# One accumulating transfer for two output tiles, and a second half that borrows the gate and up copies' tile

## The reference, cut to what matters

```
x = x + 0.5 * (silu(rms(x) @ gate1) * (rms(x) @ up1)) @ down1     # first feed-forward
x = x + mixer(rms(x))                                             # untouched
x = x + 0.5 * (silu(rms(x) @ gate2) * (rms(x) @ up2)) @ down2     # second feed-forward
y = rms(x)
```

## Time and profile of the kernel before

| what | value |
|---|---|
| median of 3 runs | 2687.12 us (2686.59 to 2691.2) |
| the profiled execution | 2686.25 us, of which its span is 2684.4 us |
| mean granted TensorE clock | 0.971 of full speed |
| TensorE matmul / VectorE / ScalarE / GpSimd busy | 95% / 64% / 50% / 11% |
| DMA: GpSimd's queue, SyncE's queue | 84.56 MB in 21.3%, 185.11 MB in 20.8% of the 16 engines' span |

### The profile page before, as it was taken

How to read it: one execution, slowest core, us unless ns; L and a number is a source line. 1 busy time by engine, 2 the same in 40 slices (tenths; PEclk the granted TensorE clock), 3 DMA queues, 4 the chain that set the end, 5 groups by cost and what they waited for, 6 DMA issues and landing times.

```text
span 2684.4 us, 52562 instructions
## 1 busy us (share of the span) xinstructions
PE 2538.3 (95%) x19577; PEld 2495.5 (93%) x19577; DVE 1710.4 (64%) x2897; ACT 1337.5 (50%) x2323; POOL 300.1 (11%) x346
## 2 busy tenths in 40 slices
PE   8999999999989999999999999999999999989997
PEld 7999999999978999999999999999999999989997
DVE  6766666666668766766666765542675666666666
ACT  5344444444447667666565664211534444444444
POOL 0012112221230000000000000000101122212220
PEclk9999999999999999999999999999999999999999
DMA  3356656555551112221221215432035656555565
GB/s 116 111 99 111 109 107 108 105 107 106 108 168 64 59 63 73 70 73 56 88 102 64 102 68 200 147 123 81 25 111 99 110 106 109 103 105 109 106 110 162
DMA packets 98984, 271.10 MB, mean 101 GB/s; under 512 B 10304, under 2 KB 16832, under 8 KB 98368
## 3 DMA queue, kind: packets, MB, share of 16 engines
q0 software_dynamic: 43648, 84.56, 21.3%
q1 hardware_dynamic: 55232, 185.11, 20.8%
HBM read 154.86 MB, written 114.77 MB: 100 GB/s over the span
## 4 chain that ended last, share of the span: by engine, by line
PE 83%; DMA 6%; DVE 5%; ACT 3%; issue 2%; POOL 0%; SPq 0%; DVEq 0%; ACTq 0%; POOLq 0%
PE banks L145 26%; PE banks L146 26%; PE banks L147 25%; DMA x_sum<-f_part 4%; DMA raw<-w_slabs 2%; PE banks L1917 1%; PE banks L1698 1%; PE banks L1708 1%; DVE mix_blk_lo L498 1%; PE banks L1710 1%; PE banks L1714 1%; DVE f_part L1039 0%; PE banks L1683 0%; DVE f_u_lo L753 0%; PE banks L1740 0%
## 5 line engine op out<-in xcount | busy, mean ns | idle before, releaser
L145 PE MATMUL banks<-f_blk_hi,f_u_hi 128*128 128x258 f32 x2496 | 709.9, 284 | 12.8 <-ACT f_snap L872 7.6
L146 PE MATMUL banks<-f_blk_lo,f_u_hi 128*128 128x258 f32 x2496 | 707.8, 284 | 0.0
L147 PE MATMUL banks<-f_blk_hi,f_u_lo 128*128 128x258 f32 x2496 | 707.0, 283 | 0.0
L145 PE MATMUL banks<-mix_blk_hi,mix_u_hi 128*128 128x258 f32 x1808 | 526.0, 291 | 2.1 <-DVE mix_blk_lo L498 0.9
L146 PE MATMUL banks<-mix_blk_lo,mix_u_hi 128*128 128x258 f32 x1808 | 511.6, 283 | 0.0
L147 PE MATMUL banks<-mix_blk_hi,mix_u_lo 128*128 128x258 f32 x1808 | 510.5, 282 | 0.0
L145 PEld LDWEIGHTS banks<-f_blk_hi,f_u_hi 128*128 128x128 f32 x2496 | 473.6, 190 | 16.3 <-issue 9.4
L146 PEld LDWEIGHTS banks<-f_blk_lo,f_u_hi 128*128 128x128 f32 x2496 | 473.4, 190 | 0.1
L147 PEld LDWEIGHTS banks<-f_blk_hi,f_u_lo 128*128 128x128 f32 x2496 | 473.5, 190 | 0.0
L145 PE MATMUL banks<-f_hb,f_u_hi 128*128 128x258 f32 x1008 | 305.6, 303 | 96.0 <-ACT f_part L880 96.0
L1208 POOL DMA_DIRECT2D x_sum<-f_part x288 | 249.3, 981 | 1036.8 <-DVE f_part L1039 762.5
(11 more groups left out here) (277 smaller groups left out, 4459.0 us busy)
## 6 DMA issues: line engine op xcount, KB each, us to landing
raw<-w_slabs SPq DMA_DIRECT2D x220, 512.0 KB, 3.5
x_sum<-f_part POOLq DMA_DIRECT2D x288, 258.0 KB, 5.4
x_sum<-x POOLq DMA_DIRECT2D x8, 1032.0 KB, 8.7
sg_kept<-sgt SPq DMA_DIRECT2D x8, 1032.0 KB, 5.8
sgs<-sg_kept SPq DMA_DIRECT2D x16, 516.0 KB, 4.7
x<-x_sum SPq DMA_DIRECT2D x2, 2752.0 KB, 13.5
x<-x_t SPq DMA_DIRECT2D x8, 516.0 KB, 8.7
x_kept<-x SPq DMA_DIRECT2D x1, 4128.0 KB, 12.1
```

The source lines that it names most:

```text
L145: pe.matmul(out, wh, xh, start=start, stop=False, skip_group_check=chained)
L146: pe.matmul(out, wh, xl, start=False, stop=False, skip_group_check=chained)
L147: return pe.matmul(out, wl, xh, start=False, stop=stop, skip_group_check=chained)
```

## The change

Five edits, made to both feed-forwards:

1. `x_sum` is laid out as 8 blocks of 128 x 1032 values, one for each half and kind. A kind's two parts q lie side by side in a row of 4128 bytes.
2. GpSimd issues one accumulating DMA for each half and kind, once both q are done: 8 in a group (516 KB each), 144 in all.
3. Kind 2 of the second half is written to `snap_t[:, 1:3]` in place of `part[2]`. So its copy waits no more for the first half's kind 2. In return the up stage's copies n = 1 and 2 wait until both transfers of kind 2 of this group are down.
4. x is copied to `x_sum` in 8 DMAs of 516 KB in place of 4 of 1032 KB.
5. The sums come back in 8 DMAs of 516 KB in place of 2: first the four that hold columns 0 to 515, then the four with columns 516 to 1031. VectorE's first addition waits for the first four, and its ninth for the other four.

```diff
@@ -56,7 +56,8 @@
 FIRST_PRODUCTS = 8
 LAST_DOWN = 3
 DOWN_PAIRS = ((3, 2), (1, 0))
-ADDED = 16 + 64 * (PAIRS - 2)
+ADDED = 32 * (PAIRS - 1)
+PARTS = ((0, 0), (1, 1), (1, 0), (0, 1))
 HIDDEN_FIRST = ((0, 0), (0, 1), (1, 0), (1, 1))
 HIDDEN = ((0, 0), (1, 1), (1, 0), (0, 1))
 DOWN_BANKS = (0, 1, 6, 7)
@@ -868,6 +869,8 @@
         act.wait_ge(s.prod, prods(i, prod_number(i, up, (0, 2, 3)[n])))
         if up:
             act.wait_ge(s.mixed, mixes(i, (1, 3, 2)[n]))
+            if n and not is_one(i):
+                act.wait_ge(k.x_added[2], i * 32 + s.added_base)
         pair = ((0, 0, 1), (2, 2, 1))[up][n]
         act.activation(halves(s.snap_t[:, n, :]), both(k, pair), ACT.Copy).then_inc(s.snap, 1)
 
@@ -875,9 +878,9 @@
 
         kind = (0, 2, 1, 3)[n]
         act.wait_ge(s.prod, prods(i, down_prod(c, (0, 2, 3, 6)[n], q)))
-        act.wait_ge(k.x_added[kind], s.added_base + (i * 64 + (32 * c - 112)))
+        act.wait_ge(k.x_added[kind], i * 32 + (s.added_base - 32 + (16 * c if kind != 2 else 0)))
         pair = DOWN_PAIRS[c ^ (n == 2)][q]
-        act.activation(halves(s.part[kind][:, q, :]), both(k, pair), ACT.Copy).then_inc(s.snap, 1)
+        act.activation(halves(part(s, c, kind)[:, q, :]), both(k, pair), ACT.Copy).then_inc(s.snap, 1)
 
     def silu(i, n):
         f, h = HIDDEN[n]
@@ -1032,11 +1035,11 @@
 
     def down_part(i, c, n, q):
 
-        part = halves(s.part[n][:, q, :])
+        to = halves(part(s, c, n)[:, q, :])
         dve.wait_ge(s.prod, prods(i, down_prod(c, (1, 4, 5)[n], q)))
         dve.wait_ge(s.snap, snaps(i, down_snap(c, (0, 2, 1)[n], q)))
         pair = DOWN_PAIRS[c ^ (n != 1)][q]
-        dve.tensor_tensor(part, both(k, pair), part, ALU.add).then_inc(s.mixed, 1)
+        dve.tensor_tensor(to, both(k, pair), to, ALU.add).then_inc(s.mixed, 1)
 
     def hidden(i, n, last):
 
@@ -1059,7 +1062,7 @@
             gt, to = halves(gt), halves(to)
         if is_one(i) and n == 0:
             for kind in range(4):
-                dve.wait_ge(k.x_added[kind], s.added_base + 16)
+                dve.wait_ge(k.x_added[kind], s.added_base + 32)
         dve.scalar_tensor_tensor(to, gt, 0.5, other, ALU.mult, ALU.mult).then_inc(s.hidden, 1)
 
     def add(first, t, m):
@@ -1067,7 +1070,7 @@
         n = 8 * t + m
         dve.wait_ge(s.down_ready, (0 if first else NT * KT) + n + 1)
         if not first and m == 0 and t < 2:
-            dve.wait_ge(k.x_back[t], s.back_base[t] + 16)
+            dve.wait_ge(k.x_back[t], s.back_base[t] + 64)
         dve.scalar_tensor_tensor(s.x[:, m, tg(t)], k.bank[DOWN_BANKS[n % 4]][:, 0:TG], 0.5, s.x[:, m, tg(t)],
                                  ALU.mult, ALU.add).then_inc(s.down_used, 1)
 
@@ -1185,28 +1188,39 @@
     s.behind_vector(dve, lambda n: add(False, *divmod(n, KT)))
 
 
+def part(s, c, kind):
+
+    return s.snap_t[:, 1:3, :] if c == 1 and kind == 2 else s.part[kind][:, :, :]
+
+
+def x_block(s, c, kind):
+
+    e, h = PARTS[kind]
+    return s.x[:, 4 * c + e:4 * c + e + 3:2, half(h)]
+
+
+def x_sum_block(s, c, kind):
+    return s.x_sum[4 * c + kind].rearrange("p (q t) -> p q t", q=2)
+
+
 def ffn_gpsimd(pool, k, s):
 
     pool.wait_ge(s.down_used, NT * KT)
+    for c in range(2):
+        for kind in range(4):
+            pool.dma_start(x_sum_block(s, c, kind), x_block(s, c, kind)).then_inc(k.x_added[kind], 16)
     for kind in range(4):
-        rows = slice(2 * kind * P, 2 * (kind + 1) * P)
-        pool.dma_start(s.x_sum[rows, :].rearrange("(m p) t -> p m t", p=P), s.x[:, 2 * kind:2 * kind + 2, :])\
-            .then_inc(k.x_added[kind], 16)
-    for kind in range(4):
-        pool.wait_ge(k.x_added[kind], s.added_base + 16)
+        pool.wait_ge(k.x_added[kind], s.added_base + 32)
 
     def group(i):
         for c in range(2):
             for kind in range(4):
-                e, h = ((0, 0), (1, 1), (1, 0), (0, 1))[kind]
-                for q in range(2):
-                    if kind < 3:
-                        pool.wait_ge(s.mixed, mixes(i, down_mix(c, kind, q)))
-                    else:
-                        pool.wait_ge(s.snap, snaps(i, down_snap(c, 3, q)))
-                    m = 2 * (2 * c + q) + e
-                    pool.dma_start(s.x_sum[m * P:(m + 1) * P, half(h)], s.part[kind][:, q, :], accum_op=ALU.add)\
-                        .then_inc(k.x_added[kind], 16)
+                if kind < 3:
+                    pool.wait_ge(s.mixed, mixes(i, down_mix(c, kind, 1)))
+                else:
+                    pool.wait_ge(s.snap, snaps(i, down_snap(c, 3, 1)))
+                pool.dma_start(s.x_sum[4 * c + kind], part(s, c, kind).rearrange("p q t -> p (q t)"), accum_op=ALU.add)\
+                    .then_inc(k.x_added[kind], 16)
 
     for i in range(2, PAIRS):
         group(i)
@@ -1251,9 +1265,9 @@
         row(PAIRS, 0, c)
     for kind in range(4):
         sp.wait_ge(k.x_added[kind], s.added_base + ADDED)
-    for t, cols in enumerate((slice(0, TG), slice(TG, T))):
-        sp.dma_start(s.x[:, :, cols], s.x_sum.rearrange("(m p) t -> p m t", p=P)[:, :, cols])\
-            .then_inc(k.x_back[t], 16)
+    for kind in (0, 2, 3, 1):
+        for c in range(2):
+            sp.dma_start(x_block(s, c, kind), x_sum_block(s, c, kind)).then_inc(k.x_back[PARTS[kind][1]], 16)
 
 
 def x_part(sp, k, n1, x_t, piece):
@@ -2753,7 +2767,7 @@
     k.x_dram = nc.dram_tensor("x_kept", (P, KT * T), F32, kind="Internal").ap()
     k.oa_dram = nc.dram_tensor("oa_kept", (HEADS, P, T), F32, kind="Internal").ap()
     k.ob_dram = nc.dram_tensor("ob_kept", (KT, P, T), F32, kind="Internal").ap()
-    x_sums = [nc.dram_tensor(f"x_sum{n}", (D, T), F32, kind="Internal").ap() for n in range(2)]
+    x_sums = [nc.dram_tensor(f"x_sum{n}", (8, P, 2 * HW), F32, kind="Internal").ap() for n in range(2)]
     k.sg_dram = nc.dram_tensor("sg_kept", (2 * KT, P, T), F32, kind="Internal").ap()
     x_t = x_t.rearrange("(m p) t -> p m t", p=P)
     y_out = y_out.rearrange("(m p) t -> p m t", p=P)
@@ -2984,7 +2998,7 @@
 
         def ffn(n):
             return dict(hidden_hi=hidden_hi, hidden_lo=hidden_lo, hid_base=8 * n, added_base=ADDED * n,
-                        back_base=(16 * n, 32 + 16 * n), x_sum=x_sums[n])
+                        back_base=(64 * n, 32 + 64 * n), x_sum=x_sums[n])
         par = stage("par", "arg exp", steps=0)
         n1 = stage("n1", "squared squared_vector added rstd_step " + HEAD, gain=G1, x=k.x1, x_loaded=x_loaded,
                    rstd_at=(2, 4), **n1_tiles)
```

## The result

The changed kernel takes 2608.78 us at the median of four runs (2604.54 to 2610.14), the kernel before took 2687.72 us (four runs, 2686.59 to 2691.2). The ratio is 0.9702, with a 95% interval of 0.9685 to 0.9718. The forecast was 2558, so 79 of the forecast 129 us came. The profiled execution took 2610.14 us, with a span of 2608.3, 76.1 less than before, and a mean granted clock of 0.983 (0.971 before).

What follows compares the result with a forecast made beforehand. It took backlogged accumulating DMAs that stall the down stage as the bound. 18 x (7.85 - 1.0) = 123.3, + 2 x 4.0, - 2 x 1.0 us: -129, so 2557, median 2558 us; range 2532 to 2672, about 8 in 10.

Steps and rivals of the forecast that it cites:

- What bounded the kernel: Down stage: copies to part wait for backlogged accumulating DMAs; 7.85 us lost a group, 5.3 idle and about 2.5 slow clock.
- The price of a long row: Accumulating DMAs: a row of 4128 bytes costs 0.41 us on one engine, between 0.33 and 0.51; a short one 0.25.
- s: Price of one 516 KB accumulating transfer in a group's queue: taken as 3.3 us, between 2.65 and 4.1.
- The queue of one group: GpSimd's accumulations: seventh transfer lands 1.9 + 7s + 2.6 us after 236.04; TensorE stands 1.0 us a group; kinds 1, 3 hidden.
- the limit on s: Highest transfer price at which the second half's kind 2 still lands by 262.6, in time for the up copy: 3.16 us.
- the halfway case: Transfer price between 3.5 and 3.85 us: up-copy stall passes 2.9 us, clock falls; 2649 us at 3.7; chance 0.18.
- rival of the slabs: Weight slab needs about 6.1 us, VectorE late to product 4's add: at most 1 to 2 us a group, 2585; no separate chance.
- The clock: TensorE: no slow clock charged for 1.0 us idle; mean granted clock to rise from 0.971 to over 0.99.
- The ends: Each feed-forward's last group: 4.0 us gained at the hidden tile's split, some 1 us of the sums' way back visible, twice.
- A price by bytes: Accumulating transfers cost 4.1 us each, the stall moves to kind 3 and the up copy: about 2703 us; slower chance 0.16.
- no stall at all: Transfer price of 3.1 us or less takes all stalls away: 2537 us; no separate chance.
- the case that had most of the chance: The forecast with its neighbours, transfer price up to 3.5 us, slabs included: 2533 to 2600 us, chance 0.62.

Runs made afterwards that it cites:

- ring_512: The changed kernel with 512 in place of 1024 bytes of descriptor space for GpSimd's DMAs: 2886.18 us, one run.
- short_rows: The changed kernel with x_sum laid out so each 516 KB transfer has 256 rows of 2064 bytes: 2907.58 us, ratio 1.0815.
- ring_768: The changed kernel with 768 in place of 1024 bytes of descriptor space for GpSimd's DMAs: 2574.53 us, one run.
- copy_first: The changed kernel with ScalarE's up copy n = 1 ahead of the split of the first hidden block: 2585.64 us, ratio 0.9623.
- vector_first: The changed kernel with VectorE's first mix and hidden block of the up stage ahead of the sums that need the slab: 2548.27 us, ratio 0.9471.
- small_slab: The changed kernel loading only 128 of 1024 columns of the gate weights' second slab in each group: 2575.03 us, ratio 0.9587.

## Why the prediction came out as it did

**What bounded the kernel: right.** The wait of the copies to `part` was a backlog of accumulations, and few can be under way at once. *ring_512* and *short_rows* show that limit by itself, as `issue` waits of GpSimd. The 7.85 us a group was the right sum to work on.

**The price of a long row: right in kind, taken too high.** The queue's share gives it, if the small packets (16 for each transfer) are counted at nothing. Before, 0.213 x 16 x 2684.4 us of engine time, less 2048 plain packets of 0.16, over 36864 rows is 0.239 us for each row of 2064 bytes. After, 0.171 x 16 x 2608.3, less the same, over 18432 rows is 0.369 us for 4128 bytes. I had taken 0.41, between 0.33 and 0.51, so s was 2.95 us and not 3.3. The price isn't a constant: by the same working a long row took 0.39 us in *ring_768* (18.4% of 2572.7) and 0.43 in *ring_512* (18.0% of 2884.4), where fewer transfers were under way, and a short one 0.24 in *short_rows* (19.7% of 2905.3) as before. The page shows 23040 packets; 18432 of them are accumulated rows, one packet each. The forecast said 25088, since I had counted the copies of x as 256 rows each, while they went as 128 of 4128 bytes.

The Trainium skill, in "Collectives: The Full Stack", section "The bandwidth ceiling: the fold count and why AG ≠ RS ≠ AR", holds that only the two sources read make an added transfer slow; from the plain row's 0.16 us that would be, as an estimate, 0.33 us for a long row and 0.16 for a short one. The runs show 0.37 and 0.24, so there is something besides, and more of it in proportion on short rows.

**The queue of one group: right.** With s = 2.95 my formula lands the seventh transfer 1.9 + 7 x 2.95 + 2.6 = 25.2 us after the first is issued. GpSimd's timeline has:

```profile
231.93 0.85 POOL L1222 DMA_DIRECT2D x_sum<-f_part  x1 [45.04 <-DVE f_part L1042]
...
247.31 0.88 POOL L1222 DMA_DIRECT2D x_sum<-f_snap  x1 [0.60 <-DVE f_snap L1042]
```

The second line is the borrowed tile's, and with the median of 10.4 us it landed at 257.7, 25.8 us after 231.93. TensorE wanted the up copy at 259.1, and from this the forecast of a small loss would have held, or none at all. Kinds 1 and 3 were hidden, as forecast (ScalarE waited for a transfer from `part` once, 1.5 us). Two small slips in the sums move nothing here: the limit on s works out at 3.15 and not 3.16, and the halfway case's 2649 leaves out the 6 us of the ends that the other cases count.

**The slab: the step that failed.** The prediction's rival of the slabs let VectorE come late to the add of product 4 only, found 2.9 us in hand there, and charged "at most 1 to 2 us a group". Two things in it were wrong. The size: it forecast 6.1 us for a slab, and it took 7.9. And, above all, the path: I followed one of the things that stand behind VectorE's wait and not all of them. Behind the sums stand the mix *and* the first hidden block; ScalarE's split waits for that block, the up copy n = 1 stands behind the split, and TensorE's product 4 needs the copy. The prediction even names "the splits of the next weights" behind ScalarE's wait, but never asks what stands ahead of the copy. The stall that it leads to is 3.0 us (2.60 in the group shown), and with the clock a group loses 4.8. Over 16 groups this is 16 x (4.8 - 1.0) = 61 us more than forecast.

The two last groups are a check of the same cause. In the last group of each feed-forward no gate stage follows, so no slab is wanted. Behind the last closing copy 14.1 and 12.1 us were gained, where the sum had 7.85 - 1.0 + 4.0 - 1.0 = 9.85. Of the 14.1, 11.8 were gained up to VectorE's first addition at the first feed-forward's end (764.26 before, 728.15 after), and 2.3 in the stretch behind it that the change hardly touches. So nearly all that such a group lost before (7.85 + 4.5) came back. The two stretches are 6.5 us better than forecast, and 1.7 came before the first period: 61 - 8 = 53 us, which is the distance of the span's gain (76.1) from the 129 forecast.

**The clock: wrong by a little, and it matters.** I charged no slow clock below 2.9 us idle. All 16 stalls of the changed kernel (2.60 to 3.57 us) were followed by half the clock, and in *copy_first* 2.05 us too. Its window, columns as above:

```profile
265.00:266.00 1.00, 1.00 (x6) 1.00 (x6) 0.97 (x2) 0.24 (x1) 0.00 (x0) 0.50 0.34 135
```

The length of the idle time alone doesn't decide: in *copy_first* the 1.75 us before 2092.38 were followed by 0.50, the 2.65 us before 200.30 by 1.00 for the next 7 us. In the changed kernel the slow clock makes a stall of 3.0 us on the average into a loss of 4.8. The forecast of a mean clock above 0.99 came out at 0.983 for this reason; it is 0.995 in *vector_first*.

**The ends.** I expected 0.5 us of TensorE's idle time left where the hidden tile is split, and 1 us of visible way back, twice. ScalarE waited 3.43 us there where it waited 6.73 before, with no idle time on TensorE, and no wait for the sums shows:

```profile
2556.46 0.63 ACT L789 ACTIVATE f_hid_hi<-f_gt 128x516 fp32r<-128x516 f32 x1 [3.43 <-DMA x_sum<-f_snap]
```

At the first feed-forward's end the way back does cost a little. The mixer's first weight slab is issued behind the eight transfers, and TensorE then waits 4.33 us (737.14) where it waited 3.92 before (772.83).

**The other rivals.** A price by bytes (4.1 us for a transfer) did not come true, and nor did the halfway case: its time (2649) isn't far from 2609, but its mechanism, the up copy waiting for the borrowed tile, is not what happened. Nearly all of the result's distance from the forecast belongs to the slab. With the slab's wait out of the way, *vector_first* measures 2548.3, in the middle of the forecast's 2558 and the 2537 for no stall at all.

**The range, and the prediction's own signs.** 2608.78 us lie inside the stated range (2532 to 2672), but not in the case that had most of the chance (2533 to 2600). The range reached so far only because it held the halfway case, whose mechanism did not occur, so that the time fell inside it is in part luck. The prediction named periods above 64 us as a sign that it is wrong, and they were 65.4. This sign is right: the path that it gave to the remaining loss was the wrong one. The other signs (kind 1, kind 3 or the up copy waiting for a transfer for more than 3 us) did not show.

**Still open.** Why a slab's packets wait for so long: 7.9 us from issue to use, where the page's median for all slabs is 3.5 and 8 turns behind a packet of 0.37 add 3.0. The slab queued just before it, issued at 242.40, may be the rest. ScalarE waited for that one until 252.02, 9.6 us:

```profile
252.02 0.64 ACT L748 ACTIVATE f_u_hi<-raw 128x512 fp32r<-128x512 f32 x1 [0.91 <-DMA raw<-w_slabs]
```

The late slab was there 5.2 us behind it. In *small_slab* the slab ahead was in use at 250.30, and the small one came 5.3 us later all the same. No run takes the slab ahead away alone. By the Trainium skill, "DMA: Bandwidth & Descriptors", section "Queues, rings and completion order", an engine takes turns between its queues packet by packet, where its packet may hold many descriptors. *small_slab* agrees as far as it goes (bytes hardly count), but no run here varies the number of packets. The price of a row and the number under way are compared only at one transfer under way: there the long rows of *ring_512* (2886.18, one run) and the short ones of *short_rows* (2907.58) are 21 us apart. Short rows with three transfers of 516 KB under way would need a larger descriptor space, and none was tried.

## What to carry to other kernels

Where a transfer is late because the DMA engines have a backlog, another buffer only moves the wait; first make the traffic cheaper, here by rows twice as long and so half the descriptors, then add the buffer. The same buffer cost 58 us with short rows and brought 40 with long ones. When traffic gets denser, look for every other transfer that shares the engines and follow *all* the work behind the instruction that waits for it, across the engines, to where TensorE needs it. Putting the work that is ready ahead of the work that waits for a slab brought 60 us by swapping four lines, and the same swap was worth 5 before the change had moved the bottleneck there.

## What the runs showed of the hardware

- An accumulating DMA has a price for each row besides its bytes: 0.24 us for 2064 bytes and 0.37 for 4128 on one engine, where a plain copy takes 0.16 for 4128. With two and with one transfer under way the long row took 0.39 and 0.43. Rows of 4128 bytes went as one packet, plain or accumulated.
- The descriptor space limits how many of GpSimd's transfers are under way, and the profile shows it only as GpSimd's `issue` wait: one transfer of 128 rows at 512 bytes of space, two at 768, three at 1024, and one of 256 rows at 1024. With one, transfers went out each 5.5 to 8.1 us, and in the window of *short_rows* the DMA engines were idle for a third of the time.
- More under way is not always better: three in place of two lengthened a slab's wait on the same engines (128.0 us in all in place of 95.6), and with it the kernel by 34 us (one run with two), until the waiting work was moved.
- Idle times of 2.60 to 3.57 us on TensorE were followed by a granted clock of 0.50 each time in the changed kernel. In *copy_first* 1.75 and 2.05 us were too, and 2.65 us once were not.
